# A hybrid decoder layer on one core: six attention units move into the last projection group, and a selection's rounds are spread anew

## The reference, cut to what matters

```python
score = einsum('bqh,bqhs->bqs', wb, relu(dots))        # indexer, block of 128 queries
_, sel = lax.top_k(score, 128)                         # 128 keys for each query
logits = einsum('bqhd,bqkhd->bqhk', qb, k_sel) * scale + bias(t5_bucket(dist))
p = softmax(where(dist >= 0, logits, -inf))
y_b = einsum('bqhk,bqkhd->bqhd', p, v_sel)
y = concat(y_a, y_b) @ w_o
```

## Time and profile before

| | us |
|---|---|
| median of 3 runs | 713.25 (711.73 to 714.31) |
| the profiled execution | 714.5 |
| its span, first to last instruction | 712.8 |
| PE busy in the span | 693.3 (97%) |
| DVE, ACT, POOL busy | 388.1, 257.1, 87.9 |
| mean granted clock of PE | 0.992 of full |

### The profile page before, as it was taken

The page is one execution under the profiler, slowest core; times in us unless marked ns, Lnnn a source line. Parts: engine busy times, 40 slices in busy tenths (PEclk is TensorE's granted clock), DMA queues, the critical chain, the costliest instruction groups (busy, mean ns, idle before and its releaser), DMA issues.

```text
span 712.8 us, 8578 instructions
## 1 busy us (share of the span) xinstructions
PE 693.3 (97%) x3472; PEld 584.6 (82%) x3472; DVE 388.1 (54%) x589; ACT 257.1 (36%) x383; POOL 87.9 (12%) x134
## 2 busy tenths in 40 slices
PE   8999999999999899999899999999999999999996
PEld 5977788888988688888898888888888888888885
DVE  3765889999579887346652433433324432212215
ACT  5556433444166376243441221331222321212212
POOL 1800220000405068102100000000000000000001
PEclk9999999999999979999999999999999999999999
DMA  8343032341511300351223323233233133132203
GB/s 257 120 148 87 33 119 67 114 146 60 178 60 59 119 1 1 119 175 62 89 67 111 100 77 118 81 98 118 64 115 118 60 118 109 69 118 86 92 0 118
DMA packets 49352, 68.59 MB, mean 96 GB/s; under 512 B 5025, under 2 KB 39841, under 8 KB 49314
## 3 DMA queue, kind: packets, MB, share of 16 engines
q1 hardware_dynamic: 44320, 60.07, 26.1%
q0 software_dynamic: 3280, 7.35, 3.1%
q10 hardware_dynamic: 1714, 0.64, 0.4%
HBM read 65.40 MB, written 4.74 MB: 98 GB/s over the span
## 4 chain that ended last, share of the span: by engine, by line
PE 85%; DVE 9%; ACT 3%; issue 2%; POOL 0%; DMA 0%; DVEq 0%; ACTq 0%
PE PS L1056 74%; PE PS L1121 2%; DVE QK L856 2%; PE PS L1248 2%; DVE A L788 1%; PE PS L1158 1%; DVE top L787 1%; PE PS L1092 1%; DVE w_lo L728 1%; PE PS L1097 1%; PE PS L1173 1%; PE PS L1145 1%; PE PS L1259 1%; DVE A L969 1%; PE PS L1098 1%
## 5 line engine op out<-in xcount | busy, mean ns | idle before, releaser
L1056 PE MATMUL PS<-hT_lo,w_hi 128*128 128x512 f32 (+2 forms) x584 | 218.2, 374 | 3.8 <-DVE hT_lo L732 2.0
L1056 PE MATMUL PS<-hT_hi,w_lo 128*128 128x512 f32 (+2 forms) x584 | 217.2, 372 | 0.0
L1056 PE MATMUL PS<-hT_hi,w_hi 128*128 128x512 f32 (+2 forms) x584 | 217.1, 372 | 0.0
L728 DVE TENSOR_TENSOR w_lo<-raw,w_hi 128x2048 fp32r<-128x2048 f32 x50 | 114.6, 2292 | 177.7 <-ACT w_hi L516 177.4
L516 ACT ACTIVATE w_hi<-raw 128x2048 fp32r<-128x2048 f32 x50 | 95.7, 1914 | 214.1 <-PE PS L1056 213.5
L1056 PEld LDWEIGHTS PS<-hT_lo,w_hi 128*128 128x128 f32 (+1 forms) x584 | 109.6, 188 | 23.6 <-DVE w_lo L728 2.7
L1056 PEld LDWEIGHTS PS<-hT_hi,w_hi 128*128 128x128 f32 (+1 forms) x584 | 109.6, 188 | 19.6
L1056 PEld LDWEIGHTS PS<-hT_hi,w_lo 128*128 128x128 f32 (+1 forms) x584 | 109.7, 188 | 18.7
L1056 PE MATMUL PS<-w_hi,ff 128*128 128x512 f32 x352 | 108.4, 389 | 0.0
L1056 PEld LDWEIGHTS PS<-w_hi,ff 128*128 128x128 f32 x352 | 66.1, 188 | 13.6
L1056 PE MATMUL PS<-w_lo,ff 128*128 128x512 f32 x176 | 68.5, 389 | 0.0
(11 more groups left out here) (162 smaller groups left out, 777.2 us busy)
## 6 DMA issues: line engine op xcount, KB each, us to landing
raw<-in_w_in_dram SPq DMA_DIRECT2D x16, 1024.0 KB, 5.5
raw<-in_w_gate_dram SPq DMA_DIRECT2D x11, 1024.0 KB, 5.3
raw<-in_w_up_dram SPq DMA_DIRECT2D x11, 1024.0 KB, 5.4
raw<-in_w_down_dram SPq DMA_DIRECT2D x11, 1024.0 KB, 4.9
raw<-in_w_o_dram SPq DMA_DIRECT2D x4, 1024.0 KB, 4.9
A<-in_x_dram SPq DMA_DIRECT2D x4, 512.0 KB, 5.5
A<-in_x_dram POOLq DMA_DIRECT2D x4, 512.0 KB, 5.3
out_dram<-A SPq DMA_DIRECT2D x8, 256.0 KB, 2.0
```

The lines of the kernel that those rows point to most:

```text
L728: dve.tensor_tensor(lo, raw_view(j), hi.bitcast(F32), ALU.subtract).then_inc(s_lo, 1)
L1056: o = pe.matmul(out, lhs[a], rhs[b], start=(first and n == 0), stop=(last and n == 2))
```

## The change

- A table `unit_order` takes the place of the nested order. Units 0 to 5 are heads 0 to 5 of block 0 as before, units 6 and 7 are heads 0 and 1 of block 1, units 8 and 9 are heads 6 and 7 of block 0, and from 10 on the order is the old one.
- The loop bodies become a function `attend(i)` on PE, DVE and ACT. Steps 0 to 5 are issued inside group 32: on PE behind each of the steps k = 2 to 7 of its 24 matmuls, on ACT and DVE ahead of the evacuation of group 32. Units 2 and 5 then write their logits to bank 6 in place of bank 0, which group 32 fills.
- Top-k: from group 24 to 28 one round to a group, from 29 to 32 two; none is left for group 32 (`topk_share`). Up to group 23 it is as it was.
- `y_hi_a` moves to i = 8 to 11, `y_lo_a` to i = 10 to 13, `y_lo_b` two steps further behind `y_hi_b`.

```diff
+    EARLY = HEADS_B - 2
+    unit_order = [(b, h) for b in range(TB) for h in range(HEADS_B)]
+    unit_order[EARLY:EARLY + 4] = [(1, 0), (1, 1), (0, EARLY), (0, EARLY + 1)]
...
+        def qk_bank(i):
+            return 6 if i % 3 == 2 and i < EARLY else QK_BANK[i % 3]
+
+        def ended(b):
+            return unit_order.index((b, HEADS_B - 1)) + 1
...
 ACT
+                if g + 1 == len(groups):
+                    for i in range(EARLY):
+                        attend(i)
                 evac(g)
...
-                if 2 <= i < 2 + HEADS_A:
-                    y_hi_a(i - 2)
+                if EARLY + 2 <= i < EARLY + 2 + HEADS_A:
+                    y_hi_a(i - EARLY - 2)
...
 DVE
+            def topk_share(g):
+                if g < G_L0 - 4:
+                    return (1, 2) if last_of_chunk(g) else (2, 1)
+                return (0, 1) if G_REC < g < first_group["ak"] else (1, 1)
...
-                if 4 <= i < 4 + HEADS_A:
-                    y_lo_a(i - 4)
+                if EARLY + 4 <= i < EARLY + 4 + HEADS_A:
+                    y_lo_a(i - EARLY - 4)
                 b = block_done(i - 1)
                 if b is not None:
                     y_norm_b(b)
-                b = block_done(i - 3)
+                b = block_done(i - 5)
                 if b is not None:
                     y_lo_b(b)
...
+                if g + 1 == len(groups):
+                    topk_rounds(48)
+                    for i in range(EARLY):
+                        attend(i)
                 evac(g)
                 if g >= G_TOPK:
-                    topk_rounds(2 if (g < G_L0 - 4 or g > G_REC) and not last_of_chunk(g) else 1)
+                    topk_rounds(topk_share(g)[0])
...
                 if g >= G_TOPK:
-                    topk_rounds(2 if (g < G_L0 - 4 or g > G_REC) and last_of_chunk(g) else 1)
-            topk_rounds(48)
+                    topk_rounds(topk_share(g)[1])
+            for i in range(EARLY, UNITS + PV_LAG):
+                attend(i)
...
 PE
+            def beside(g):
+                if len(indexer_beside(g)):
+                    return lambda k: indexer_dot(g, k)
+                if g + 1 == len(groups):
+                    return lambda k: attend(k + EARLY - KT) if k >= KT - EARLY else None
+                return None
...
-                    if i in (1, 2):
-                        evacuated(pe, len(groups) - (4, 1)[i - 1])
+                    if i == 1:
+                        evacuated(pe, len(groups) - 4)
+                    elif i == EARLY + 2:
+                        evacuated(pe, len(groups) - 1)
...
-            for i in range(UNITS + PV_LAG):
+            for i in range(EARLY, UNITS + PV_LAG):
+                attend(i)
```

More of the change, by code:

```diff
@@ L270, in block_done @@
         def block_done(i):
-            b, h = divmod(i - PV_LAG, HEADS_B)
-            return b if h == HEADS_B - 1 and 0 <= b < TB - 1 else None
+            if not 0 <= i - PV_LAG < UNITS:
+                return None
+            b, h = unit_order[i - PV_LAG]
+            return b if h == HEADS_B - 1 and b < TB - 1 else None
+        def qk_bank(i):
+            return 6 if i % 3 == 2 and i < EARLY else QK_BANK[i % 3]
+        def ended(b):
+            return unit_order.index((b, HEADS_B - 1)) + 1
         def indexer_beside(g):
@@ L1087, in project @@
                     feature_group(w, m, IKW if kind == "ikw" else P, g % 4, 0, S, s_proj,
-                                  (lambda k: indexer_dot(g, k)) if len(indexer_beside(g)) else None)
+                                  beside(g))
             def turn(src, bank):
@@ L1204, in _ @@
                 feature_group(w_split(0), m, P, m, S // 2, S, s_proj)
-            for g in range(2, len(groups)):
-                project(g)
-                if g in LEVEL_AT:
-                    level(LEVEL_AT[g])
-                elif g == G_DIAG:
-                    diagonals()
-                elif g == G_OFF:
-                    between_chunks()
-                elif g == G_REC:
-                    recurrence_out()
-                elif g == G_YTURN:
-                    turn_y()
             def turn_y_b(b):
@@ L1223, in turn_y_b, with attend @@
                 o.then_inc(s_ybt, 1)
-            for i in range(UNITS + PV_LAG):
+            def attend(i):
                 if i < UNITS:
-                    b, h = divmod(i, HEADS_B)
+                    b, h = unit_order[i]
                     if i == 0:
@@ L1257, in _ @@
                         pe.wait_ge(s_pts[u % 2], u // 2)
-                    for s in range(u // HEADS_B + 1):
+                    for s in range(unit_order[u][0] + 1):
                         o = pe.transpose(PS[:, 2 + u % 2, s * P:(s + 1) * P], Pb[u % 4][:, s * P:(s + 1) * P],
@@ L1264, in _ @@
                     turn_y_b(b)
+            for g in range(2, len(groups)):
+                project(g)
+                if g in LEVEL_AT:
+                    level(LEVEL_AT[g])
+                elif g == G_DIAG:
+                    diagonals()
+                elif g == G_OFF:
+                    between_chunks()
+                elif g == G_REC:
+                    recurrence_out()
+                elif g == G_YTURN:
+                    turn_y()
+            for i in range(EARLY, UNITS + PV_LAG):
+                attend(i)
             def row_block(j, k0, acts, t, first, last):
```

119 lines of the change are left out of this document (61 added, 58 removed).

## The result

| | before | changed |
|---|---|---|
| median, us | 712.57 (711.73 to 714.31, 4 runs) | 718.85 (717.76 to 721.11, 4 runs) |
| ratio, 95% interval | | 1.0083 (1.0066 to 1.0100) |
| the profiled execution, its span | 714.5, 712.8 | 721.11, 719.4 |
| mean granted clock | 0.992 | 0.985 |

The forecast was 712.3 us with a range up to 716.3. The changed kernel takes 718.9: about 6 us more than before, and 2.5 us over the range's end.

The account below looks back on a forecast made before the run. PE (85% of the chain) was taken as the bound, with DVE as full from 200.3 to 249.4 us. Terms +0.4 at unit 20 and -1.4 behind it make -1.0: 713.25 becomes 712.3 us, range 710.0 to 716.3.

Parts of the forecast that it names:

- `y_lo_a` beside POOL: Four `y_lo_a` beside POOL's 256-key tiles take longer: +0.4 us at unit 20, with 0 and +1.2 as ends.
- units 6 to 19: DVE sets the pace, 10.0 us up to unit 16's maximum; unit 20 at 270.2, the three units lost won back.
- The walk to the first maximum: DVE's new order followed from 200.39 us to unit 0's first maximum at 250.3, against 249.48 before.
- The waits ahead of groups 29 and 31: PE's waits for DVE's low part of a key chunk both go, -1.8 us for PE.
- The stall in group 32: PE stands at unit 3 from 244.6 to 250.8 for `nm` of unit 0, 6.3 us idle.
- The half clock behind it: After PE's 6.3 us idle in group 32, 1.2 GHz for about the first 3 us of work.
- The serial piece: Unit 5's maximum, exp and turned copy, then group 32's evacuation until 258.3; unit 8 waits, +3.1 us there.
- The block ends: From unit 20 on, waits for finished blocks 1 and 2 shrink: -1.4 us (1.1 and 0.3).
- Half clock up to unit 20: Rival: clock falls again or never rises behind unit 8's wait; +2 to +5 us, 715.7; chance 0.23.
- The shorter piece: Rival: ACT and DVE meet unit 5 sooner or the clock returns at 252; unit 8 at 256.8, 710.6 us; chance 0.18.
- no stall: Rival: DVE reaches unit 0 by 244.6, PE loses none of 6.3 us in group 32; 706 us; chance 0.06.
- the later `y_lo_b` wins nothing: Rival: the change does nothing, as PE is the bound there anyway; 714 us; chance 0.07.

Follow-up runs that it names:

- e2: The changed kernel with POOL's multiplication of the recurrence's output cut into eight pieces of 256 columns; 716.29 us, ratio 1.0041.
- e9: The changed kernel with 32 useless matmuls in PE's long wait inside group 32, run once more for its profile; 717.9 us in one run.
- e16: The changed kernel with ACT's turned copy of unit i-3 ahead of its exp of unit i; 718.17 us, ratio 1.0064.
- e4: The kernel before with only `y_lo_b` two steps later; 710.27 us, ratio 0.9952.
- e13: The changed kernel with 32 useless matmuls inside group 32 and eight more meant for the wait ahead of unit 8; 719.32 us, ratio 1.0088.
- e1: The changed kernel with the old shares of the top-k rounds; 709.28 us, ratio 0.9948.

## Why the prediction was wrong, step by step

At unit 20 I expected 270.6 (270.2 and 0.4 for `y_lo_a` beside POOL) and the trace has 276.95. The 6.3 us come from two steps: a split of DVE that took 2.4 us longer than booked, and 3.8 us in units 6 to 19, where I had them won back.

**The walk to the first maximum: 2.4 us too early, a mis-sized term.** I had "ACT's split ends at ... 216.9, DVE's at 219.2". The split of DVE started at 216.90, but took 4.74 us and not 2.2. The walk is right up to there to 0.1 us (idle 1.04, 0.62, 3.09 where I had 1.0, 0.5, 3.1) and the first maximum came at 252.74, not 250.3. All of the difference is this one instruction, and e2 shows the cause by turning it round. The rule that I cited from the Trainium skill (SBUF — State Buffer, "Who interferes with whom") states just this exclusion, and the trace agrees, 4.74 against 2.29 us. I held it only against the `y_lo_a` and didn't ask what POOL does at 216.9, although the kernel before has its 3.62 us there; the list of POOL in the same microseconds would have told. The waits ahead of groups 29 and 31 went as forecast, but for 0.31 us.

**The stall in group 32** is 8.52 for the 6.3 forecast, which is those 2.4 less the 0.3 kept ahead of group 29. The mechanism was right, and no cover existed. The half clock behind it I took for 3 us of work; it held until 257.4, four microseconds of work, and cost 1.7 us (e9).

**The serial piece** was right: exp, copy, 1.2 us of ACT, 1.39 of DVE; the evacuation ended at 260.87, 2.6 after my 258.3, of which 2.4 had come with the first maximum. The wait ahead of unit 8 was 1.55, within the 1 to 2 announced.

**Units 6 to 19: 3.8 us too early, the step that failed outright.** "The three units lost are won back" took DVE as never idle and PE as free to follow it at once. Unit 8 was 5.9 us late and unit 20 was 6.7: nothing was won back. DVE in order of time, then ACT:

```profile
264.91 0.42 DVE L940 CUSTOM_DVE_ANT_0 A<-PS,A 128x256 f32<-128x256 f32 x1 [1.37 <-PE PS L1131]
...
268.68 1.23 DVE L914 TENSOR_TENSOR hT_lo<-A,hT_hi 128x512 fp32r<-128x512 f32 x1
269.84 0.41 DVE L940 CUSTOM_DVE_ANT_0 A<-PS,A 128x256 f32<-128x256 f32 x1
...
273.20 0.55 DVE L940 CUSTOM_DVE_ANT_0 A<-PS,A 128x384 f32<-128x384 f32 x1
```

```profile
270.48 0.51 ACT L640 ACTIVATE A<-A,nm 128x256 f32<-128x256 f32 x1 [1.25 <-DVE nm L942]
...
270.99 0.36 ACT L643 ACTIVATE A<-PS 128x256 f32<-128x256 f32 x1
```

From the evacuation's end to the end of unit 16's maximum it is 13.0 us (260.87 to 273.9) where I summed 10.0. 1.4 of them is idle time ahead of the maximum of unit 10, for logits that PE issued late. 0.9 is the `y_lo_a`: from start to start they hold DVE for 0.89, 0.60, 1.16 and 0.60 us, where I had four times 0.6 and booked 0.4 elsewhere. 0.7 is the maximum of unit 16 itself, which my ten maxima leave out. Then unit 20 followed 3.0 us behind that maximum and not 1.9. The 3.0 and this 1.1, less the 0.4 booked, are 3.7. In the kernel before it was no shorter (maximum at 266.67, unit 20 at 270.24, which is 3.6 us from start to start, 3.75 in the changed kernel), so its own rows would have told.

My only link from DVE to PE was `nm` of unit i-3. There are two more. The product of unit 10 needs ACT's copy of unit 10, which stands behind ACT's exp of unit 13 (270.48), which needs the maximum of unit 13 (269.84), behind a `y_lo_a` of 1.23 us: the wait of 1.60 us at 271.40. And `turn_y_b` needs DVE's normalization, 272.60 to 273.29. In the changed kernel both end at nearly the same time. e16 took the first out, and the second held unit 20 almost where it was.

e2 takes the first step out, and what it leaves is the second: counted from the start of POOL's multiplication, unit 20 stands at 58.48 us in e2 and at 54.33 before, 4.15 us later, where the forecast had 0.4.

**The block ends:** -1.4 forecast, -1.6 measured (unit 20 to the output projection 24.16 us, before 25.76). e4 gives the whole edit as 3.4 us in the time and 2.7 in S, where my terms held 2.3 (0.94 and 1.4).

**The rivals.** "Half clock up to unit 20" had the sign and nearly the size (715.7, up to 718), and its sign shows up: the clock did fall a second time at unit 8, as it says. But it was back at 267.6, nine microseconds before unit 20, and its mechanism isn't what held PE: from the maximum of unit 10 to that of unit 16 e9 and e13 run alike at either clock. Ahead of unit 10 it stays open, with 1.5 us as its most. That it came near the measured time is luck. The shorter piece and "no stall" didn't come. That the later `y_lo_b` wins nothing is refuted by e4.

Put together by parts: the new shares cost 4.2 us alone and 8.7 in S beside the other two (76.57 in e1, 85.24 changed); the late `y_lo_b` wins 3.4; the units bring 0 to 1 with DVE in time (not clear of the noise) and cost about 3 when it is late.
